# Moving the constant tables of a one-core Trainium2 kernel in front of its large SBUF tiles

## What is computed

```
for i in range(2):                                  # first block
    hl, hc = modulate(xl, ...), modulate(xc, ...)   # 512 and 256 tokens
    if i == 0: oc, ol = mla_pool_mixer(hc, hl, ...) # latent attention and pooling
    else:      oc, ol = gqa_mixer(hc, hl, ...)      # grouped attention
    xl = xl + ml[:, 2] * ol
    xl = xl + ml[:, 5] * conv_ffn(modulate(xl, ...), w_up, conv_w, conv_b, w_down)   # D_FF = 2816
    ...                                             # the same for xc where i == 0
x = rms_norm(xl, g_final)
x = x + rms_norm_2(gmlp_mixer(rms_norm_2(x, ...), ...), ...)                 # second block
x = x + rms_norm_2(dilated_attention_mixer(rms_norm_2(x, ...), ...), ...)
```

## Time and profile before

| | us |
|---|---|
| median of 3 runs | 2686.58 (2681.17 to 2686.64) |
| the profiled execution, its own time | 2685.14 |
| its span, first to last instruction | 2683.5 |
| TensorE matmul busy | 2607.3 (97%) |
| VectorE busy | 1798.9 (67%) |
| ScalarE busy | 1152.5 (43%) |

### The profile page before, as it was taken

One profiled execution on the slowest core, in us unless ns is written; L12 is line 12 of the kernel. 1 busy time (PEld: TensorE's weight loads), 2 busy tenths in 40 slices (PEclk: granted clock), 3 DMA queues, 4 the chain that ended last, 5 costly groups with the idle time before them and its releaser, 6 DMA issues. The chain is left out here.

```text
span 2683.5 us, 38325 instructions
## 1 busy us (share of the span) xinstructions
PE 2607.3 (97%) x15122; PEld 2212.3 (82%) x15122; DVE 1798.9 (67%) x2906; ACT 1152.5 (43%) x1949; POOL 109.1 (4%) x125
## 2 busy tenths in 40 slices
PE   7989999999999999999999999999999999999998
PEld 4868788899999978888999987888877788778776
DVE  6566536666666667877888875766577565665675
ACT  3255525433333334655555543432254333343343
POOL 1110001100000000000000010000010000000001
PEclk9999999999999999999999999999999999999998
DMA  6440113433333311021333324222322322222221
GB/s 241 154 135 17 32 48 118 152 115 111 108 106 109 104 53 49 24 72 56 110 103 117 104 84 136 87 87 89 92 81 79 89 81 82 87 81 71 88 81 47
DMA packets 67892, 246.88 MB, mean 92 GB/s; under 512 B 7696, under 2 KB 8240, under 8 KB 67056
## 3 DMA queue, kind: packets, MB, share of 16 engines
q1 hardware_dynamic: 52896, 188.88, 22.2%
q0 software_dynamic: 14688, 55.20, 6.3%
q10 hardware_dynamic: 144, 0.52, 0.1%
HBM read 242.33 MB, written 2.24 MB: 91 GB/s over the span
## 5 line engine op out<-in xcount | busy, mean ns | idle before, releaser
L2825 DVE TENSOR_TENSOR WL<-RAW,WH 128x1024 fp32r<-128x1024 f32 (+1 forms) x197 | 241.6, 1228 | 231.9 <-ACT WH L2035 230.5
L1035 PE MATMUL PS<-AB,BH 128*128 128x384 f32 (+1 forms) x1256 | 388.8, 310 | 3.7 <-DVE BL L2832 2.4
L1035 PE MATMUL PS<-HM,WH 128*128 128x512 f32 x968 | 387.0, 400 | 0.9 <-ACT DG L2035 0.8
L1037 PE MATMUL PS<-AB,BL 128*128 128x384 f32 (+1 forms) x1256 | 387.1, 308 | 0.0
L1036 PE MATMUL PS<-AB,BH 128*128 128x384 f32 (+1 forms) x1256 | 386.6, 308 | 0.0
L1037 PE MATMUL PS<-HM,WL 128*128 128x512 f32 x968 | 380.5, 393 | 0.0
L1036 PE MATMUL PS<-HM,WH 128*128 128x512 f32 x968 | 379.7, 392 | 0.0
L2035 ACT ACTIVATE WH<-RAW 128x1024 fp32r<-128x1024 f32 (+1 forms) x197 | 208.0, 1057 | 248.3 <-PE PS L1037 247.9
L1035 PEld LDWEIGHTS PS<-AB,BH 128*128 128x128 f32 x1256 | 235.8, 188 | 9.3 <-DVE GATED L3325 4.7
L1036 PEld LDWEIGHTS PS<-AB,BH 128*128 128x128 f32 x1256 | 236.3, 188 | 1.1 <-issue 0.5
L1037 PEld LDWEIGHTS PS<-AB,BL 128*128 128x128 f32 x1256 | 236.2, 188 | 0.0
(11 more groups left out here) (471 smaller groups left out, 5346.5 us busy)
## 6 DMA issues: line engine op xcount, KB each, us to landing
RAW<-in_tiles SPq DMA_DIRECT2D x298, 512.0 KB, 3.5
MRAW<-in_mods POOLq DMA_DIRECT2D x80, 512.0 KB, 4.7
RAW_M<-in_tiles SPq DMA_DIRECT2D x34, 512.0 KB, 3.6
TB<-bias_rows POOLq DMA_DIRECT2D x16, 576.0 KB, 6.4
FIRST<-in_mods SPq DMA_DIRECT2D x8, 1024.0 KB, 17.4
X_M<-in_x SPq DMA_DIRECT2D x2, 1024.0 KB, 6.0
VN_GB<-in_gm_rows POOLq DMA_DIRECT2D x2, 1024.0 KB, 6.4
out_x<-X_M SPq DMA_DIRECT2D x8, 256.0 KB, 2.0
```

The source lines that it names most:

```text
L1035: pe.matmul(out_, wh, xh, start=first, stop=False, skip_group_check=True)
L1037: return pe.matmul(out_, wl, xh, start=False, stop=last, skip_group_check=True)
L2825: dve.tensor_tensor(WL[:, s.mod(2), 0:width], RAW[:, s.mod(2), 0:width], f32(WH[:, s.mod(2), 0:width]), ALU.subtract).then_inc(tile_split[ ...
```

## The change

The nine small tables move in front of X_M, and the sum of their sizes is rounded up to 64. The two pads of 32 bytes go. CONST and LN stay behind MRAW. No instruction is added, removed or moved: both programs have the same 20,525 instructions in the same order with the same waits, and only the addresses in them differ.

```diff
+    ONES = keep("ONES", [P, P])
+    IDENT = keep("IDENT", [P, P])
+    MOD = keep("MOD", [P, 96, 2])
+    CVEC = keep("CVEC", [P, KC, 2])
+    SCALE1 = keep("SCALE1", [P, KC, 2])
+    STAT = keep("STAT", [P, 2, 8])
+    COLS = keep("COLS", [P, N_COLS])
+    CVEC_AMID = keep("CVEC_AMID", [P, MOD_ROWS * (KC + 1)])
+    PICK = keep("PICK", [P, MOD_ROWS])
+    cur[0] = -(-cur[0] // 64) * 64
     X_M = keep("X_M", [P, KC, TM])
     x_c_at = cur[0]
     X_C = keep("X_C", [P, KC, TC])
     RAW = keep("RAW", [P, 2, D])
-    cur[0] += 32
     wh_at = cur[0]
     WH = keep("WH", [P, 2, D], F32R)
     wl_at = cur[0]
     WL = keep("WL", [P, 2, D], F32R)
-    cur[0] += 32
     mraw_at = cur[0]
     MRAW = keep("MRAW", [P, 2, D])
-    MOD = keep("MOD", [P, 96, 2])
-    COLS = keep("COLS", [P, N_COLS])
-    CVEC = keep("CVEC", [P, KC, 2])
-    CVEC_AMID = keep("CVEC_AMID", [P, MOD_ROWS * (KC + 1)])
-    PICK = keep("PICK", [P, MOD_ROWS])
-    ONES = keep("ONES", [P, P])
-    IDENT = keep("IDENT", [P, P])
-    SCALE1 = keep("SCALE1", [P, KC, 2])
     CONST = keep("CONST", [P, 64])
-    STAT = keep("STAT", [P, 2, 8])
     LN = keep("LN", [P, 4, 24])
     scratch = cur[0]
```

## The result

The changed kernel takes 2712.7 us, the median of 4 runs (2711.5 to 2717.2), against 2686.6 us for the kernel before in 4 runs on the same chip: a ratio of 1.0103 [1.0091, 1.0114]. The forecast was 2670.5, with a range of 2645 to 2708. The sign was wrong and the range missed the time.

The account below looks back on a forecast made before the run. TensorE's step from matmul to matmul was taken as the bound; -11.4 us (512 columns) and -8.2 (256) made -19.6, of which -16 arrives: 2669.1, plus 1.5 for the runs' median, 2670.5 us; range 2645 to 2708.

Parts of the forecast that it names:

- TensorE's steps bound the kernel, and a step has a level that the place of its operands sets: All matmuls: time follows the step from one to the next, whose possible levels depend on the distance of operand addresses.
- Tables, VectorE, DMA: 0: Small tables' addresses, VectorE's subtractions and DMA: no cost, 0; 1 us if the cover of RAW and WH were gone.
- The start at 0 is worth nothing: Operands starting on a 64-byte piece: no gain, as FIRST6 and FIRST7 both took 1.06 us for 16 records.
- rival 3: All matmuls: a start at 0 saves a 64-byte piece, 6.67 ns each; 56 us, four fifths arriving, 2641 us; chance 0.08.
- 128 lies nearer to 0 than 192 does: Weak reason for lower levels at 512 and 256 columns: remainder 0 has the lowest 512-column level, 192 the highest.
- 512 columns: -7 ns x 1628 = -11.4 us: Triples at 512 columns with weights in staging: from 687 to 680 ns, 1628 of them, -11.4 us.
- Rival 2: Main triples lock at the upper level, 700 ns at 512 columns, +21.2 us, 4.4 more at 256; 2711 us; slower 0.30.
- 256 columns: -8.2 us: Second feed-forward part, 628 triples at 256 columns: from 353 to 340 ns, -8.2 us.
- 384 columns left at 0: 628 triples at 384 columns: no change in the forecast; 12.6 us either way allowed in the low and high ends.
- HR left at 0: 128 triples with moving WH and weights HR: no change in the forecast; -2.6 us allowed at the low end.
- Four fifths arrive: Whole kernel: of the -19.6 us gain only -16 us reaches the time, since TensorE is partly idle or waiting.
- Rival 1: Nothing happens: levels come from the rhythm of the waits, not from addresses; 2686.6 us; chance 0.20.

Follow-up runs that it names:

- d320_start0: Changed kernel with CVEC, SCALE1 and STAT put behind MRAW again, staging and arena still at 0 (mod 64): 2685.6 us, ratio 0.9999 to the kernel before.
- d128_start32: Kernel before with CVEC, SCALE1 and STAT put in front of X_M, pads and start at 32 (mod 64) kept: 2707.8 us, ratio 1.0078.

## Why the prediction was wrong

- *TensorE's steps bound the kernel, and a step has a level that the place of its operands sets.* Right, and shown by the mirror pair: the same table bytes, on one side or on the other of the staging tiles, are worth 0.8 to 1.0%.
- *Tables, VectorE, DMA: 0.* Right: 1228 and 688 ns, the busy time of VectorE is 1.4 us more over 2906 instructions, and d320_start0, with the new start and six of the nine tables in their new places, is at 0.9999.
- *The start at 0 is worth nothing.* Right, and with it rival 3 (a piece saved per matmul, 2641 us) falls: d320_start0 for the gain, d128_start32 for the loss.
- *"128 lies nearer to 0 than 192 does", so the lower levels.* This is the step that failed. It took the remainder as a scale on which levels grow, from two known points. Measured, the long triple is 683.6 at 0, 687.5 to 687.7 at 64, 697.7 to 698.4 at 128 and 699.5 at 192: 128 is close to the highest level. My own reading of "two streams in step" gave no order of the levels, and I put one in by nearness. On the right period before is at 64, after at 128 and HR, at minus 64 before, at 192: 128 is as far from the level of 687 as from that of 700, and nearness would have chosen neither.
- *512 columns: -7 ns x 1628 = -11.4 us.* Measured 698.4 - 687.7 = +10.7 ns, x 1628 = +17.4 us. Rival 2 had +13 ns and +21.2.
- *256 columns: -8.2 us.* Measured +3.4 ns x 628 = +2.1 us for AB, and GA with 176 triples, which I hadn't costed by itself, +10.8 ns each, +1.9.
- *384 columns left at 0.* They did move, 520.0 to 527.8, x 628 = +4.9 us; I had kept this for the ends of the range alone, because the shape showed one level only. One level seen at one remainder says nothing of another.
- *HR left at 0.* -2.6 ns x 128 = -0.3 us. These terms give 17.4 + 2.1 + 1.9 + 4.9 - 0.3 = 26.0. That the table's last column gives the same is in part luck: it counts unbroken triples only, in which the groups of the 1628 grew by 15.5 us, and it has HC and GC at 256 columns (+1.5 us), which the sum leaves out.
- *Four fifths arrive.* The other way round: 26.0 us in unbroken triples came with 30.7 us of busy time and 28.6 of span. Nothing of a longer step was hidden, and some 4 us lie at stretches of the lower clock, of which the changed kernel's profiled execution had more; that part is none of the change's steps.
- *Rival 2* had the place (the main triples), the mechanism (the upper level) and nearly the time: 2711 against 2712.7. It had too much at 512 columns and nothing at 384, and that the two errors cancel is luck. The range ended at 2708 because I counted half of its chance below 2705.
- *Rival 1* rested on two levels at equal addresses. Those are real: AB at 256 columns has 113.3 and 117.8 ns in one kernel and at one remainder. At 512 columns they are the finer effect. At 256 they are as large as what the remainder does: 353.3 and 340.6 ns a triple at 320 and 64.

The rows said before any run that the place matters. The Trainium skill, "TensorE: Matmul & The Clock Gate", section "Step-by-step: what each phase is for", says that TensorE has two independent SBUF read ports and that loading the next weights doesn't steal read bandwidth from the running matmul. From that I drew that the distance is worth nothing, and these runs disagree: 226.8 to 233.4 ns a step for one shape, at one clock, with one order of instructions, by the distance. The measurement decides.

What is shown is the dependence: on moving minus weights address, for float32r with a load of 128x128 ahead of each matmul; on a period of 256 bytes at 512 and 384 columns, and with its sign at 512. That the two reads meet inside SBUF is argued and stays so. Why a step pays, and what picks between two levels at one remainder, is open.

## What to carry to other kernels

When a float32r matmul kernel is bound by TensorE and loads weights for each matmul, treat the remainder on 256 of (moving address - weights address) as a tuning value: here 0 and 64 were good (0 where runs of one shape are long), 192 cost 0.3%, 128 cost 0.8 to 1.0%, and 96, the one odd multiple of 32 that was tried, cost 1.4%. Any small tile that moves across the operands changes it, so compare the step from matmul to matmul in unbroken runs, before and after a change of layout; a matmul's own mean duration (for HM with WH at L1036 392 ns before, 395 ns at the same place after) isn't what it costs. And where a measured quantity takes a few levels by an address, don't interpolate between them: a layout with another remainder is a new case until it has run.

## What the runs showed of the hardware that was not expected

- At 512 columns the step is 226.8 to 227.1 ns at remainder 0, 228.9 to 229.0 at 64, 232.3 to 233.3 at 128, 233.3 at 192 and 233.4 at 96. Columns / 2.4 GHz is 213.3, so even the best layout is 13.5 ns over it.
- These are steps in long runs of one shape. At remainder 0 the first two triples of GA with BH behind another shape take 697 and 690 ns before 680 sets in, and most of GM with WH, which alternate with 256 columns, stay at 695 to 697. At 128 the 244 steps of WH with HR are 228 to 233 ns but for 34 of 241 ns.
- At 384 columns it is 173.3 ns (0 and 64) against 176.0 (128) and 176.7 (96), over 160.0. At 256 columns it is 113.3 to 120.0, over 106.7, and the order is another one: 0 is best at 512 columns and worst at 256.
- With equal addresses a stretch can hold 113.3 or 117.8 ns at 256 columns, and change after an interruption.
- The start of the tiles within 64 bytes is worth nothing that could be measured where both operands have the same start: 0.9999 [0.9982, 1.0015] at remainder 320, and 1.0103 [1.0091, 1.0114] against 1.0078 [1.0056, 1.0100] at 128, two intervals that overlap.
